# Seven-product feed-forward: weight sums staged in PSUM, remainders split between VectorE and GpSimd; the down projection from tiles that are split once

## The reference

```python
D_MODEL, SEQ, D_FF = 1024, 512, 2816
...
hffn = modulate(rmsnorm(x, g_norm2[l]), shift2, scale2)
a, u = jnp.split(jnp.einsum('bsd,df->bsf', hffn, w_ffn_in[l]), 2, axis=-1)
x = x + gate2[:, None, :] * jnp.einsum('bsf,fd->bsd', jax.nn.silu(a) * u, w_ffn_out[l])
return rmsnorm(x, g_final)
```

## Time and profile before

| what | value |
|---|---|
| median of three executions | 2131.59 us (2130.89 to 2136.7) |
| profiled execution, its own time | 2134.38 us |
| its span in the trace | 2132.6 us |
| PE busy, share of the span | 2037.6 us, 96% |
| PEld, DVE, ACT, POOL busy | 79%, 54%, 44%, 45% |
| DMA mean | 95 GB/s |

### The profile page before, as it was taken

How to read it: one execution, slowest core, us unless ns; L and a number is a source line. 1 busy time by engine, 2 the same in 40 slices (tenths; PEclk the granted TensorE clock), 3 DMA queues, 4 the chain that set the end, 5 groups by cost and what they waited for, 6 DMA issues and landing times.

```text
span 2132.6 us, 31113 instructions
## 1 busy us (share of the span) xinstructions
PE 2037.6 (96%) x11334; PEld 1692.8 (79%) x11334; DVE 1146.2 (54%) x1395; ACT 944.3 (44%) x1187; POOL 956.3 (45%) x430
## 2 busy tenths in 40 slices
PE   9999999999999999688889989998999999999999
PEld 5888878787878788688888868777798778888887
DVE  4344424445454545887776564886663347555312
ACT  4566652423232343433335426767744335444321
POOL 3322234343434343455565434867457233444443
PEclk9999999999999999898999999999999999999999
DMA  8121123333333322222223222220134122322331
GB/s 331 60 68 62 50 89 124 133 127 114 128 113 136 109 89 79 69 79 79 79 79 99 89 79 70 89 70 23 60 102 158 57 79 75 102 93 94 99 109 60
DMA packets 56105, 202.87 MB, mean 95 GB/s; under 512 B 6224, under 2 KB 8400, under 8 KB 54608
## 3 DMA queue, kind: packets, MB, share of 16 engines
q1 hardware_dynamic: 56016, 201.65, 28.4%
HBM read 199.53 MB, written 2.10 MB: 95 GB/s over the span
## 4 chain that ended last, share of the span: by engine, by line
PE 32%; DVE 10%; issue 9%; ACT 4%; POOL 4%; DVEq 0%; ACTq 0%; POOLq 0%
PE acc L2347 4%; PE acc L2349 4%; PE acc L2348 4%; POOL w_lo L576 3%; PE aux L2347 2%; PE aux L2349 2%; PE aux L2348 2%; DVE wc_lo L1677 2%; PE aux L2744 1%; PE aux L2777 1%; PE aux L2778 1%; PE aux L2774 1%; DVE raw L1665 1%; DVE tn L1664 1%; PE aux L2746 1%
## 5 line engine op out<-in xcount | busy, mean ns | idle before, releaser
L576 POOL TENSOR_TENSOR w_lo<-raw,w_hi 128x1024 fp32r<-128x1024 f32 x315 | 776.9, 2475 | 1110.2 <-ACT w_hi L648 1109.4
L648 ACT ACTIVATE w_hi<-raw 128x1024 fp32r<-128x1024 f32 x315 | 330.9, 1059 | 616.3 <-PE acc L2349 313.2
L2347 PE MATMUL acc<-x_hi,w_hi 128*128 128x512 f32 (+1 forms) x1016 | 399.5, 393 | 7.8 <-DVEq L1346 3.6
L2349 PE MATMUL acc<-x_hi,w_lo 128*128 128x512 f32 (+1 forms) x1016 | 393.0, 387 | 0.0
L2348 PE MATMUL acc<-x_lo,w_hi 128*128 128x512 f32 (+1 forms) x1016 | 392.7, 386 | 0.0
L2347 PEld LDWEIGHTS acc<-x_hi,w_hi 128*128 128x128 f32 x1016 | 191.3, 188 | 51.9 <-DVEq L1346 5.7
L2349 PEld LDWEIGHTS acc<-x_hi,w_lo 128*128 128x128 f32 x1016 | 191.1, 188 | 39.5
L2348 PEld LDWEIGHTS acc<-x_lo,w_hi 128*128 128x128 f32 x1016 | 191.4, 188 | 37.4 <-issue 0.5
L2744 PE MATMUL aux<-x_hi,w_hi 128*128 128x256 f32 x160 | 52.7, 329 | 48.4 <-DVE tn L1731 34.4
L1388 DVE SCALAR_TENSOR_TENSOR adac<-ada,c_act,adac 128x1024 f32<-128x1024 f32 x28 | 39.4, 1407 | 93.7 <-DMA ada<-in_ada 93.2
L614 POOL TENSOR_TENSOR cfy<-cfy,tn 128x512 f32<-128x512 f32 x51 | 69.6, 1364 | 22.1 <-ACT tn L648 19.5
(11 more groups left out here) (610 smaller groups left out, 4753.9 us busy)
## 6 DMA issues: line engine op xcount, KB each, us to landing
raw<-in_weights SPq DMA_DIRECT2D x322, 512.0 KB, 3.5
ada<-in_ada SPq DMA_DIRECT2D x32, 512.0 KB, 3.7
ada<-in_ada_first SPq DMA_DIRECT2D x8, 1024.0 KB, 12.2
resid<-in_x SPq DMA_DIRECT2D x2, 1024.0 KB, 6.3
out<-resid SPq DMA_DIRECT2D x16, 128.0 KB, 1.8
decay<-in_tables SPq DMA_DIRECT2D x4, 256.0 KB, 3.6
memf<-in_mem SPq DMA_DIRECT2D x1, 1024.0 KB, 4.8
angles<-in_tables SPq DMA_DIRECT2D x1, 512.0 KB, 5.1
```

Source lines behind the costliest of these rows:

```text
L576: nc.gpsimd.tensor_tensor(lo_home(u), raw[s][:], hi_home(u).bitcast(F32), ALU.subtract).then_inc(lo_ready, 1)
L648: return nc.scalar.activation(out, in_, func, **kw)
L2347: M(out, a_hi, b_hi, start=first, stop=False)
L2349: return M(out, a_lo, b_hi, start=False, stop=last)
```

## The change

The weight sums of a tile (all but one, the fourth) are now staged in PSUM, in the two banks `acc[:, 0:2T]`, which hold no other tile at that time. To get there ACT first copies one block of unit b into PSUM (`copy_block`). POOL's second job per tile shrinks to one 512-wide remainder, DVE's grows to a 1024-wide one whose source is in PSUM. DVE's order per tile now starts with `middle`. Two of the input sums are staged in PSUM as well. For the down projection each hidden tile is split once: the high parts go into the places that the scheme no longer needs (`h_high`), the low parts overwrite `hf` in place (`h_low`). Outputs 0 to 3 go depth by depth, then outputs 4 to 7 one after the other over all 22 depths. `by_depth` orders the weight units on the host accordingly; their number and bytes stay.

```diff
-DOWN_RING = 12
-DOWN_AT = (("acc", 0), ("acc", 1), ("aux", 3), ("aux", 4), ("aux", 5), ("aux", 0), ("aux", 1), ("aux", 2))
+DOWN_AT = (("acc", 0), ("acc", 1), ("aux", 3), ("aux", 4), ("aux", 2), ("aux", 0), ("aux", 1), ("aux", 5))
+FAST_BANKS = ((3, 1, 4), (0, 2, 5))
...
+        sums12 = acc[:, 0:2 * T]
+        early_sum = [aux[:, 3 * T:5 * T].rearrange("p (k n) -> p k n", k=HALF_K),
+                     aux[:, T:3 * T].rearrange("p (k n) -> p k n", k=HALF_K)]
...
-                    nc.gpsimd.tensor_tensor(wc_lo[n][:, T:3 * T], sum24[:], wc_hi[n][:, T:3 * T].bitcast(F32),
+                    nc.gpsimd.tensor_tensor(wc_lo[n][:, 2 * T:3 * T], sum4, wc_hi[n][:, 2 * T:3 * T].bitcast(F32),
...
+            def copy_block(u):
+
+                s = u.slot(RING)
+                act.wait_ge(raw_loaded[s], (u.div(RING).val() + 1) * 16)
+                own["oraw_ready"].own(f(sums12[:, 0:T], raw[s][:, 0:T]))
...
             split_hi(At(ff0 + 3))
+            operand_hi(t_hi[:, 0, :, :], early_sum[0], 2)
+            operand_hi(t_hi[:, 1, :, :], early_sum[1], 0)
             act.wait_ge(unit_used, ff0 + 1)
             gate_tile(bank(At(0)))
             nc.scalar.sem_inc(acc_free[0], 1)
+            copy_block(At(ff0 + 5))
             split_hi(At(ff0 + 4))
             split_diff(At(ff0 + 5))
...
                     first_product(n)
+                    own["sum_split"].next()
+                    copy_block(u + 1)
                     split_hi(u)
+                    fast_gate(n)
                     split_diff(u + 1)
-                    fast_gate(n)
-                    split_sums(At(done + 4 * n + 4, i, 8), n)
+                    two_sums_hi(n, At(done + 4 * n + 4, i, 8))
+                    last_sum_hi(n)
...
+                step.own(V.tensor_tensor(s1, b[:, T:2 * T], s1, ALU.add))
+                step.own(V.tensor_tensor(s2, s1, a[:, 0:T], ALU.subtract))
...
+                own["sum_made"].own(V.tensor_tensor(b[:, 0:T], b[:, T:2 * T], s2, ALU.subtract))
                 if again:
                     own["pair_split"].next()
+                own["pair_made"].own(V.tensor_tensor(sum4, a[:, T:2 * T], s2, ALU.subtract))
...
+                own["sum_split"].own(V.tensor_tensor(wc_lo[n][:, 0:2 * T], sums12, wc_hi[n][:, 0:2 * T].bitcast(F32), ALU.subtract))
...
                     u = At(ff0 + 2 * FAST + 4 + 2 * n, i, 4)
-                    first_sums(u, n)
                     middle(n, i * 2 + (FAST + n))
-                    last_sums(u, n)
-                    ending(n, i * 2 + (FAST + n))
+                    first_sums(u)
+                    whole(n)
+                    last_sums(u)
+                    hidden(i * 2 + (FAST + n), at_tile(hf, i * 2 + (FAST + n)), fast_banks(n)[0])
                     sum_low(n)
...
-            for x in range(3):
-                down_low(x)
+            for k in range(6):
+                down_low(k)
             middle(1, FT - 1)
...
+            next_at = {14: (0, 1), 15: (2, 3), 17: (4,), 20: (5,), 23: (6,), 24: (7,)}
+            for j in range(4, 25):
+                for k in range(4 * j - 10, min(4 * j - 6, FT)):
+                    down_hi(k)
...
+            for n in range(4, KT):
+                for k in range(FT):
+                    at_ = (n - 4) * FT + k
+                    if at_ % KT == 0 or k == 0:
+                        wh, wl = weights(At(d0 + FT // 2 + at_ // KT))
+                    m = three(ffn_bank(n), wt(wh, at_ % KT), wt(wl, at_ % KT), h_high(k), h_low[:, k, :], k == 0, k == FT - 1)
```

More of the change, by code:

```diff
@@ L311, in build_program, with h_high @@
         xf = hf[:, FT - KT:FT, :]
[L312 to L321, removed]
+        h_low = put("h_low", (P, FT, T), F32R, where=over)[0]
+        sum4 = spare[:]
+        def h_high(k):
+            kind, at_ = ((wc_hi0, wc_lo0, wc_hi1, wc_lo1)[k // 3], k % 3) if k < 12 else ((t_hi, t_lo)[(k - 12) // 6], k % 6)
+            flat_ = kind[:] if k < 12 else kind[:].rearrange("p a k n -> p (a k n)")
+            return flat_[:, at_ * T:(at_ + 1) * T]
         (qkvf, sgate, cfin, cfy, gb, gbt, egr, kb, kdec, bt, dect, xt3, gcols), _ = overlay(
@@ L975, in _ @@
             fast_gate(1)
-            for x in range(3, 10):
-                down_hi(x)
             own["nega_ready"].own(f(nega[0:GDN_H, 0:1], cols[0:GDN_H, C0["a_log"]:C0["a_log"] + 1], ACT.Exp))
@@ L1667, in last_sums @@
-            def last_sums(u, n, again=True):
-                a = raw[u.slot(RING)]
+                own["oraw_ready"].next()
+                step.own(V.tensor_tensor(s1, b[:, T:2 * T], s1, ALU.add))
+                step.own(V.tensor_tensor(s2, s1, a[:, 0:T], ALU.subtract))
+            def last_sums(u, again=True):
+                a, b = raw[u.slot(RING)], raw[(u + 1).slot(RING)]
+                s2 = sums12[:, T:2 * T]
+                own["sum_made"].own(V.tensor_tensor(b[:, 0:T], b[:, T:2 * T], s2, ALU.subtract))
@@ L1685, in hidden, with operand_low @@
+            def operand_low(out, src, hi, at_):
+                dve.wait_ge(S["sum_hi"], at_)
+                own["sum_split"].own(V.tensor_tensor(out, src, hi.bitcast(F32), ALU.subtract))
             def hidden(k, src, gate):
@@ L1737, in middle, with whole @@
                     b.rearrange("p (a n) -> p a n", a=2), ALU.add))
-            def ending(n, k):
+            def whole(n):
                 a, b, c = fast_banks(n)
@@ L1759, in down_low @@
                 own["tile_hi"].next()
-                own["tile_split"].own(V.tensor_tensor(down_ring(False, x), hf[:, x % FT, :], down_ring(True, x).bitcast(F32),
-                                                   ALU.subtract))
+                own["tile_split"].own(V.tensor_tensor(h_low[:, k, :], hf[:, k, :], h_high(k).bitcast(F32), ALU.subtract))
             middle(0, FT - 2)
-            ending(0, FT - 2)
-            for x in range(3):
-                down_low(x)
+            whole(0)
@@ L1767, in _ @@
+            hidden(FT - 2, at_tile(hf, FT - 2), fast_banks(0)[0])
+            for k in range(6):
+                down_low(k)
             middle(1, FT - 1)
-            ending(1, FT - 1)
+            whole(1)
+            hidden(FT - 1, at_tile(hf, FT - 1), fast_banks(1)[0])
             g_f = cols[:, C0["g_final"]:C0["g_final"] + KT]
@@ L2749, in _ @@
             made = RET_H * RET_VT + KT
-            own["sum_split"].next(3)
-            own["sum_split"].skip()
+            own["sum_split"].next()
+            own["sum_split"].skip(3)
             with loop(pe, (FT - FAST) // 2, [(own["pair_split"], 2), (own["sum_split"], 2), (own["bank_free"], 4)]) as i:
@@ L2768, in _ @@
                     own["bank_free"].next()
+                    own["pair_split"].next()
                     product(b[:, h1], wc_hi[n], wc_lo[n], 2, "b22").then_inc(S["tile_done"], 1)
-            def down_part(x, n, wh, wl, at_, last, used=False):
-                k, out, hi, lo = x % FT, ffn_bank(n), down_ring(True, x), down_ring(False, x)
-                m = M(out, wt(wh, at_), hi, start=k == 0, stop=False)
-                if used:
-                    m.then_inc(S["down_used"], 1)
-                M(out, wt(wh, at_), lo, start=False, stop=False)
-                return M(out, wt(wl, at_), hi, start=False, stop=last)
             wait_bank(At(t_ret + 94))
```

206 lines of the change are left out of this document (83 added, 123 removed).

## The result

| | before | after |
|---|---|---|
| median, us | 2132.09 (2130.89 to 2136.7, 4 runs) | 2073.01 (2070.84 to 2076.3, 4 runs) |
| ratio to before, 95% interval | | 0.972 (0.970 to 0.9741) |
| profiled execution, its span | 2134.38, 2132.6 | 2076.3, 2074.5 |
| mean granted clock | 0.982 | 0.993 |

The change takes off 59 us in the medians and 58 in the profiled executions. A table by stretches of the span says where. "Input" is the end of VectorE's last `x_lo` ahead of the stage, "tile 2" and "tile 20" the starts of its first operation after those tiles' last product (L1743 before, L1748 after), "seam" the stretch from the second block's first product to the product behind the four statistics matmuls.

The account below looks back on a forecast made before the run. Taken as bound: PE, stalled in the loop by blocked VectorE operations. Loop 49.2 + start 5.5 - last tile 3.8 + seam 11 = 62 us off 2134.4 profiled gives 2072.4, median 2069, range 2058 to 2100.

Parts of the forecast that it names:

- What bounds the loop: Seven-product loop: PE waits because two VectorE operations sit out POOL's, ordered ahead of what PE wants; 34.4 us of waits.
- The loop at 10.0 us per tile: Loop of 19 tiles: bound by PE at 10.0 us each instead of 12.59, 49.2 us gained.
- The start: Stage start to tile 2's end: PE starts 10.2 us earlier, tile 2 ends at 894.5 not 900.0, 5.5 gained.
- The last tile: Tile 21: six low parts ahead of the last middle, a 2.2 us wait plus 1.6 of lower clock, 3.8 lost.
- The down projection: Down projection: 528 matmuls in 123 us before and 528 after, nothing gained or lost.
- The seam: Between the blocks: no wait ahead of the statistics, 17.5 us becomes 6.5, 11 gained; statistics matmuls 3.7 us.
- The sum: Whole kernel: loop, start, last tile and seam together gain 62 us.
- (b): Loop: single staging buffer's round trip through ACT and DVE just misses PE; 11.5 us per tile, 2098 us, chance 0.18.
- (c): Loop: PSUM operands don't spare DVE POOL's turn; two blocked add 4 us, 13.5 per tile, 2136 us; chance 0.04.
- (d): New start or second pass: an unseen wait gives back most of the loop's gain, within 0.3%; chance 0.03.
- same: Whole kernel: outcome of no measurable change, within 0.3% or 6.4 us; chance 0.02.

Follow-up runs that it names:

- sums_in_sbuf: Changed kernel with its two staged weight sums in SBUF instead of PSUM, every order as changed: 2102.42 us, 0.987 of before.
- reorder_only: Kernel before with one edit, middle ahead of the weight sums in the loop, sums still in SBUF: 2107.62 us, 0.9891 of before.
- psum_old_order: Changed kernel with its first two weight sums ahead of middle again in the loop: 2083.87 us, 0.9782 of before.
- low_2x: Changed kernel with VectorE's 1024-wide low part made twice in each loop tile: 2072.67 us, 0.9727 of before.
- low_4x: Changed kernel with VectorE's 1024-wide low part made four times in each loop tile: 2137.1 us, 1.0021 of before.
- down_only: Kernel before with the new down projection alone, loop and start as they were: 2121.27 us, 0.9961 of before.
- after_again: Changed kernel unaltered, timed again beside other versions on the same chip: 2072.11 us, 0.9723 of before.
- middle_early: Kernel of both_moves_again with tile 2's middle ahead of tile 3's last sums and low part, loops rotated: 2063.01 us, 0.967 of before.
- both_moves_again: Changed kernel with ScalarE's first gate ahead of the input sums' high parts and three low parts, not six, ahead of the last middle: 2063.85 us, 0.9674 of before.

## Why the prediction held, point by point

**What bounds the loop: held.** VectorE's order and two blocked operations. sums_in_sbuf shows the blocking by itself (1.43 us per tile), reorder_only the order by itself on the kernel before (1.47) and psum_old_order on the changed one (0.61). What the prediction did not say is how the two interact; either alone leaves waits.

**The loop at 10.0 us per tile: held (9.94).** The 1024-wide low part, which no row showed, took 1.22 where 1.25 was taken. The free time ahead of L1736 is 1.21 us where 1.0 was worked out, and from L1736's end to PE's b21 there are about 0.8 more. low_2x uses 1.22 us of these 2.0 and loses almost nothing, low_4x asks for 3.7 and waits 2.1. No PSUM surcharge shows in the operations of a tile: the groups above have 0.69 with an operand there and 0.69 without.

**The start, 5.5 predicted, 4.7 measured.** PE's first product came as worked out (10.0 earlier, 10.2 said). The term mis-sized is the time from there to tile 2's end: 22.3 us where 872.8 to 894.5, 21.7, were said. The wait of b21 for `middle` behind tile 3's sums is there, 3.96 us, and b21 starts when it was said (895.82, less the 5.9 us by which the input is late, is 889.9, where about 890 was said). The two products behind it take 5.4 us to the end of the tile, at the lower clock, where 4.5 were allowed.

**The last tile, 3.8 predicted, 2.2 measured.** The wait was right to 0.03 us; the 1.6 us of lower clock behind it, taken from the stalled tiles, did not come. This is the one term whose mechanism was absent in the changed kernel. It isn't an idle term: behind the same wait of 2.24 to 2.25 us it came in down_only, sums_in_sbuf and psum_old_order, 1.5 us each. Whether it comes was not foreseen, and is not explained by these runs. Of the 2.5 us by which loop and last tile together gave more than predicted, 1.6 are this and 1.1 are the 9.94 for 10.00, less 0.2 for a tile 21 of 10.2 without its wait.

**The down projection, 0: held** to 0.01 us in the changed kernel; the 2.3 us that it was shorter in three of the experiments is in no term.

**The seam, 11 predicted, 11.7 measured.** No wait ahead of the statistics. They took 3.0 us (1218.21 to 1221.24), not 3.7: mis-sized by 0.7.

**The sum.** 62 us predicted, 64.3 in these stretches, 59 in the medians (57.6 in the comparison with after_again). The difference of stretches and medians is within what the unchanged stretch ahead scatters. That all three lie so close is in part luck: the sum was taken from one profile in which the stalled loop ran at 12.72 us per tile, and the same loop code ran at 12.20 in down_only, 9.4 us less over the 18 tiles.

**The rivals.** (b), the round trip of the single staging buffer, did not occur, and 1.22 us more of VectorE's work per tile did not bring it on (low_2x). (c), VectorE blocked in spite of the PSUM operand, did not occur. Its price for two blocked operations was too high as well: with the sums in SBUF two were blocked, by 2.8 us and not 4, and the tile took 11.37, not 13.5, since the wait stayed at 1.0 to 1.4 us and the clock at 1.00. (d) did not occur: the last tile's wait gives back 2.2 us and the waits of the start are inside its term. The chances were put together 0.01 off: (d) alone has 0.03, and "same" was given 0.02.

## What to carry to other kernels

Where an engine waits for VectorE, look first for operations of it that take a multiple of their width's time beside GpSimd: putting one operand into free PSUM banks made them short again here, and in the changed kernel was worth more than the better order (25.7 us against 11.0). Reordering alone moves a stall to the next queue; follow what then stands behind the slow operations, on other engines too. Test the cover with a repeated operation before trusting or spending it, since the price of more work is not linear: here 1.2 us more per tile cost nothing, and 3.7 more cost 3.8. And check a mark taken from one engine against the engine that it stands for: in two of the versions VectorE's first operation behind a tile came 3.3 and 4.4 us after PE's last matmul of tile 2.

## What the runs showed of the hardware that was not expected

**The price of a short wait.** Recurring waits of 1.04 to 1.40 us in every tile (sums_in_sbuf) left the granted clock at 1.00:

```profile
934.00:1070.00 136.00, 121.73 (x1005) 119.37 (x1005) 112.86 (x120) 63.35 (x84) 83.85 (x36) 1.00 0.29 93
```

Recurring waits of 1.85 to 2.31 us (low_4x) came with 0.88 and 1.7 us more per tile. A single longer wait behind a loop comes out both ways. One of 2.23 us in tile 21, after 190 us without one, did not lower the clock (after; the same in after_again and low_2x). One of 2.24 or 2.25 us in the same place did, to 0.61 or 0.62 over the next 4.4 us, where the loop ahead had waits of 1.04 to 1.40 us (sums_in_sbuf), of 0.68 to 1.94 (down_only), or of no more than 0.5 (psum_old_order). And one of 1.8 us at the start was followed by the lower clock in middle_early and not in both_moves_again. What decides it is not shown by these runs; a term for it should carry both ends.

**VectorE's widths with an operand in PSUM.** 0.69 us for 512 and 1.22 for 1024 elements of fp32, the same as from SBUF where POOL is idle. The Trainium skill (VectorE: DVE Perf Modes, the section on the TRN2 errata) also gives, for the fp32 add with N elements, (N + 151) cycles at 0.96 GHz, measured at 512 and 2048. An estimate by it is 0.69 us for 512 and 1.22 for 1024. These rows agree with it for both places, and the page's larger fixed cost for PSUM does not show.
